# Cumulated decays of a gated delta rule: spread by four-row matmuls on four row tiles, subtracted on ScalarE, masked on GpSimd, two chunks earlier

## What is computed

```python
gcum = jnp.cumsum(gc, axis=-1)
idx = jnp.arange(c)
tril = idx[:, None] >= idx[None, :]
diff = gcum[..., :, None] - gcum[..., None, :]
decay = jnp.where(tril, jnp.exp(jnp.where(tril, diff, 0.0)), 0.0)
a_mat = jnp.where(strict, jnp.einsum("bhnid,bhnjd->bhnij", kb, kc) * decay, 0.0)
intra = jnp.einsum("bhnid,bhnjd->bhnij", qc, kc) * decay
```

## Time and profile before

| | |
|---|---|
| runs | 581.05, 581.10, 581.26 us; median 581.1 |
| profiled execution | 581.15 us, its span 579.3 us |
| TensorE busy | 568.1 us, 98% of the span |
| VectorE busy | 382.2 us, 66% |
| ScalarE busy | 299.0 us, 52% |
| GpSimd busy | 78.2 us, 13% |

### The profile page before, as it was taken

How to read it: one execution, slowest core, us unless ns; L and a number is a source line. 1 busy time by engine, 2 the same in 40 slices (tenths; PEclk the granted TensorE clock), 3 DMA queues, 4 the chain that set the end, 5 groups by cost and what they waited for, 6 DMA issues and landing times.

```text
span 579.3 us, 10011 instructions
## 1 busy us (share of the span) xinstructions
PE 568.1 (98%) x4010; PEld 504.7 (87%) x4010; DVE 382.2 (66%) x612; ACT 299.0 (52%) x470; POOL 78.2 (13%) x93
## 2 busy tenths in 40 slices
PE   9999999999999999989999999999999999999997
PEld 8999999899788999878888888898788888888886
DVE  4778898855666652977754573757766566566664
ACT  5569555515435456647464634366454544545542
POOL 4011210761600000163321000000000000000000
PEclk9999999999999999999999999999999999999999
DMA  8954477595755425433443455565466756667631
GB/s 255 256 179 142 151 189 248 98 301 175 208 148 163 137 83 192 146 107 112 152 141 116 146 176 202 162 193 168 145 188 178 216 177 187 185 180 217 167 125 72
DMA packets 101432, 98.25 MB, mean 170 GB/s; under 512 B 4819, under 2 KB 87816, under 8 KB 101387
## 3 DMA queue, kind: packets, MB, share of 16 engines
q1 hardware_dynamic: 99072, 93.69, 52.8%
q0 software_dynamic: 1808, 2.78, 2.7%
q10 hardware_dynamic: 506, 1.14, 0.6%
HBM read 96.46 MB, written 1.84 MB: 170 GB/s over the span
## 4 chain that ended last, share of the span: by engine, by line
PE 88%; DVE 6%; issue 3%; ACT 2%; POOL 1%; DVEq 0%; ACTq 0%; POOLq 0%
PE ps L1423 18%; PE ps L1425 17%; PE ps L1424 17%; PE ps L1521 13%; PE ps L1524 6%; PE ps L1601 4%; PE ps L1428 4%; PE ps L1441 2%; DVE w_lo L944 2%; PE ps L1498 2%; PE ps L1756 1%; PE ps L1730 1%; PE ps L1632 1%; ACT w_hi L623 1%; DVE cacc L1039 1%
## 5 line engine op out<-in xcount | busy, mean ns | idle before, releaser
L944 DVE TENSOR_TENSOR w_lo<-raw,w_hi 128x2048 fp32r<-128x2048 f32 x76 | 176.3, 2319 | 99.2 <-ACT w_hi L623 99.0
L623 ACT ACTIVATE w_hi<-raw 128x2048 fp32r<-128x2048 f32 x76 | 145.3, 1912 | 81.5 <-PE ps L1425 75.2
L1521 PE MATMUL ps<-h_both,w_hi 128*128 128x512 f32 x352 | 122.8, 397 | 1.0 <-DVE w_lo L944 0.6
L1423 PE MATMUL ps<-h_both,w_hi 128*128 128x256 f32 x352 | 101.7, 289 | 0.7 <-DVE h_both L970 0.3
L1424 PE MATMUL ps<-h_both,w_hi 128*128 128x256 f32 x352 | 99.5, 283 | 0.0
L1425 PE MATMUL ps<-h_both,w_lo 128*128 128x256 f32 x352 | 99.5, 283 | 0.0
L1524 PE MATMUL ps<-h_both,w_lo 128*128 128x256 f32 x352 | 91.1, 279 | 0.0
L1521 PEld LDWEIGHTS ps<-h_both,w_hi 128*128 128x128 f32 x352 | 63.9, 188 | 15.1 <-issue 3.2
L1423 PEld LDWEIGHTS ps<-h_both,w_hi 128*128 128x128 f32 x352 | 67.3, 191 | 5.0 <-issue 4.8
L1524 PEld LDWEIGHTS ps<-h_both,w_lo 128*128 128x128 f32 x352 | 66.4, 189 | 3.3
L1424 PEld LDWEIGHTS ps<-h_both,w_hi 128*128 128x128 f32 x352 | 67.4, 192 | 0.0
(11 more groups left out here) (359 smaller groups left out, 965.6 us busy)
## 6 DMA issues: line engine op xcount, KB each, us to landing
raw<-in_w_in SPq DMA_DIRECT2D x31, 1024.0 KB, 5.2
raw<-in_w_gate SPq DMA_DIRECT2D x22, 512.0 KB, 4.0
raw<-in_w_up SPq DMA_DIRECT2D x22, 512.0 KB, 5.3
raw<-in_w_down SPq DMA_DIRECT2D x11, 1024.0 KB, 4.9
raw<-in_cmp_w SPq DMA_DIRECT2D x8, 1024.0 KB, 6.3
raw<-in_w_proj_a SPq DMA_DIRECT2D x4, 1024.0 KB, 5.3
raw<-in_w_proj_b SPq DMA_DIRECT2D x4, 1024.0 KB, 5.1
raw<-in_w_out SPq DMA_DIRECT2D x4, 1024.0 KB, 5.1
```

What stands on the lines that cost most here:

```text
L623: nc.scalar.activation(w_hi[s % NSPL][:], raw[RAW_OF[n]][:], ACT.Copy).then_inc(hi_done, 1)
L944: nc.vector.tensor_tensor(w_lo[s % NSPL][:], raw[RAW_OF[n]][:], w_hi[s % NSPL][:].bitcast(f32), ALU.subtract).then_inc(lo_done, 1)
L1423: pe.matmul(bank, lhs(lh), rhs(rh), start=start, stop=False)
L1521: cross = lambda stop: pe.matmul(banks[part][:], hi[:, k, part * P:(part + 1) * P], h_both[:, :, k, :], start=(k == 0), stop=stop)
```

## The change

Five things change together.

1. **Sums as rows.** `decay_columns` gets four more matmuls, each with a group's four columns of `g` as the stationary side and `upper` as the moving one. They leave the cumulated decays of four problems as rows, at partitions 32b to 32b+3 of `ps7`. VectorE copies them into `gc_rows` with four copies, in slot 6.
2. **Spreading.** The stage `row` moves from half 1 of slot 12 to half 1 of slot 10, behind the sums of squares. Its sixteen matmuls now have four rows each: a column of `sel4` (ones and zeros) repeated 128 times, and `gc_rows`. Group b uses the rows 32b and up of the array and a bank of its own (`row_ps`, banks 2 to 5), and the groups take turns, the quarter q being the outer loop.
3. **Difference.** It moves from VectorE to ScalarE: sixteen activations, Relu with scale -1 and the column `gc` as bias. The exponential takes scale -1 in turn, and stands in slot 12 between the SiLU of chunk 10 and that of chunk 11, behind `decay_factors`.
4. **Mask.** `negmask` is gone, with its load. GpSimd multiplies `ET` with `upper`, four products, ahead of the bias rows' transfer; the scaling waits for them.
5. `stage_columns` on VectorE now follows the convolution of chunk 11.

Core of the diff:

```diff
-STAGE_AT = {("kc", 0, 1): "row", ("vc", 0, 0): "kt", ("vc", 0, 1): "vt", ...
+STAGE_AT = {("gv", 2, 1): "row", ("vc", 0, 0): "kt", ("vc", 0, 1): "vt", ...
...
-            sp.dma_start(negmask[:], c_negmask).then_inc(const_in, 16)
...
+            for b in range(NB):
+                pool.wait_ge(et_ready, b + 1)
+                nc.gpsimd.tensor_tensor(problems(ET, b), problems(ET, b), upper[:].unsqueeze(1).to_broadcast([P, 4, P]), ALU.mult).then_inc(et_masked, 1)
             pool.wait_ge(conv_done, 12)
...
             for b in range(NB):
-                pool.wait_ge(et_ready, b + 1)
+                pool.wait_ge(et_masked, b + 1)
...
+            def decays():
+                for b in range(NB):
+                    wait_use(act, "row", b)
+                    nc.scalar.activation(problems(ET, b), problems(ET, b), ACT.Exp, scale=-1.0).then_inc(et_ready, 1)
...
                     if name == "row":
-                        act.wait_ge(done, u // GRING + 1)
-                        nc.scalar.activation(problems(ET, b), problems(ET, b), ACT.Exp).then_inc(et_ready, 1)
+                        act.wait_ge(g_mm, u + 1)
+                        rows4 = row_ps[b][:].rearrange("p (q c) -> p q c", q=4)
+                        for q in range(4):
+                            ins = nc.scalar.activation(problems(ET, b)[:, q, :], rows4[:, q, :], ACT.Relu, scale=-1.0, bias=pcol("gc", b)[:, q:q + 1])
+                        ins.then_inc(done, 1)
...
-                for k in {FIRST_STAGE_SLOT: [n - 2, n - 1]}.get(n, [n - 2] if 2 <= n < FIRST_STAGE_SLOT else []):
-                    conv_step(k)
+                if 2 <= n <= FIRST_STAGE_SLOT:
+                    conv_step(n - 2)
+                if n == FIRST_STAGE_SLOT:
+                    decay_factors()
+                    decays()
+                    conv_step(n - 1)
...
             def decay_factors():
                 dve.wait_ge(pre_pe, 5)
+                for b in range(NB):
+                    nc.vector.tensor_copy(gc_rows[32 * b:32 * b + 4, :], ps[7][32 * b:32 * b + 4, 0:P]).then_inc(rows_cum, 1)
...
-                    if name == "row":
-                        for q in range(4):
-                            ins = nc.vector.scalar_tensor_tensor(problems(ET, b)[:, q, :], b4[:, q, :], pcol("gc", b)[:, q:q + 1],
-                                                                 negmask[:], ALU.subtract, ALU.add)
-                        ins.then_inc(done, 1)
-                        if b == NB - 1:
-                            stage_columns()
...
                     if (n, half) == (FIRST_STAGE_SLOT, 0):
                         conv(n - 1)
+                        stage_columns()
...
+                for b in range(NB):
+                    last = pe.matmul(ps[7][32 * b:32 * b + 4, 0:P], pcol("g", b), upper[:], start=True, stop=True)
                 last.then_inc(pre_pe, 1)
...
+            def decay_rows():
+                pe.wait_ge(rows_cum, NB)
+                pe.wait_ge(sel_done, 1)
+                for q in range(4):
+                    for b in range(NB):
+                        group = slice(32 * b, 32 * b + 4)
+                        last = pe.matmul(row_ps[b][:, q * P:(q + 1) * P], sel4[group, q:q + 1].to_broadcast([4, P]), gc_rows[group, :],
+                                         start=True, stop=True)
+                        if q == 3:
+                            last.then_inc(g_mm, 1)
...
-                    if name == "row":
-                        pe.wait_ge(pre_dve, 5)
-                        if b == 0:
-                            pe.wait_ge(rk_ready, 1)
-                        for q in range(4):
-                            last = mm(q, pcol("g", b)[:, q:q + 1].to_broadcast([P, P]), upper[:])
```

More of the change, by code:

```diff
@@ L288, in hybrid_block @@
         csum_n = at("csum_n", cursor[0] - 2 * KB, [P, 2 * SEQ])
-        ident, upper, negmask = own("ident", [P, P]), own("upper", [P, P]), own("negmask", [P, P])
+        ident, upper, gc_rows = own("ident", [P, P]), own("upper", [P, P]), own("gc_rows", [P, P])
         vcz = at("vcz", yb_at + 12 * KB, [P, 4, DH])
@@ L1574, in head_sums @@
                     if j == 2:
+                        wait_use(pe, "row", NB - 1)
                         pe.wait_ge(nq_sq, 4)
@@ L1592, in head_sums @@
                     last.then_inc(csum_tr, 1)
+            def decay_rows():
[8 more added lines that the diff above has]
+                            last.then_inc(g_mm, 1)
             def gdn(name):
+                if name == "row":
+                    decay_rows()
+                    return
                 for b in range(NB):
```

24 lines of the change are left out of this document (11 added, 13 removed).

## The result

The changed kernel takes **587.75 us** (587.67 to 588.0) against 581.1 (581.05 to 581.26): ratio 1.0112, 95% interval 1.0098 to 1.0125, slower by 6.65 us. The profiled execution has a span of 585.9 us, 6.6 more than before.

What follows compares the result with a forecast made beforehand. TensorE, busy 568.1 of 579.3 us, was taken as the bound. Added work and stalls 1 and 2, less 3.81 us, left it 1.9 us behind; masks and stall 3 made 5.7: 581.1 + 5.7 = 586.8 us, range 583.2 to 589.8.

Steps and rivals of the forecast that it cites:

- The slack of chunk 12, and the split behind sixteen activations: ScalarE before chunk 12: 4.2 us of activations make its high part 6.2 us late against a slack of 1.6.
- TensorE's own costs: TensorE: 0.35 us added in slot 6; row stage 1.2 us (ends 0.95 and 3.8) in place of 3.81.
- Stalls 1 and 2: TensorE waits 3.1 us before chunk 12 for its split, and 1.05 us before chunk 13 for VectorE.
- The masks and the port: VectorE's last convolution beside GpSimd's masks: SBUF port shared, 0.79 us lost per product, 3.2 for four.
- Stall 3: Before chunk 14: TensorE waits 1.2 us for GpSimd's `flat`, out at 117.9, so chunk 14 is 5.7 us late.
- The table loads that I cost at nothing: ScalarE: load back to SiLU, 1.28 us, and one before the compressed branch's softmax; both hidden, 1.3 us if the latter uncovered.
- Two sums of the rivals: Forecast totals for the free port, 583.8 us, and for the faster case, 1.3 us gained, 579.8 us.
- the port doesn't bind: Rival at the last convolution: VectorE and GpSimd run side by side, total 583.8 us; chance 0.15.
- The row tiles run one after another: Rival in TensorE's row stage: no overlap, everything 2.6 us later, total 589.4 us; chance 0.08.
- The clock: Rival on TensorE: clock falls behind a 3.1 us stall, losing 2.5 us, total 589.3 us; chance 0.09.
- Faster: Rival at ScalarE: four banks cleared inside chunk 12's slack, 1.3 us gained, total 579.8 us; chance 0.03.

Runs made afterwards that it cites:

- r1_split_first: Changed kernel with the sixteen activations moved on ScalarE behind chunk 12's high part and the SiLU of chunk 9: 582.46 us, ratio 1.0022.
- r4_group_order: Changed kernel with the sixteen row matmuls in group order, four on one row tile and then four on the next: 587.63 us, ratio 1.011.
- r5_keep_clock: Changed kernel with fifteen identity matmuls added in TensorE's wait before the last four transposes of the keys: 586.73 us, ratio 1.0098.
- r9_chain_first: r6 with GpSimd's clearing of DTb and scalings of kn put behind the transfers out of the diagonal blocks: 578.82 us, ratio 0.9965.
- r3_mask_as_write: Changed kernel with GpSimd's four mask products replaced by four memsets of a free tile, so another output: 585.52 us, ratio 1.0073.
- r2_no_mask: Changed kernel with GpSimd's four mask products left out, so another output: 582.97 us, ratio 1.0036.
- r8_masks_last: Changed kernel with GpSimd's order alone changed: scalings of two groups, `flat`, then masks and the other scalings: 585.53 us, ratio 1.0076.
- r11_tiles_only: Kernel before with the row tiles alone, stage still in slot 12, VectorE subtracting and adding negmask: 581.07 us, ratio 0.9999.
- r6: Changed kernel with both the split ahead of the activations (r1_split_first) and GpSimd's order of r8_masks_last: 581.33 us, ratio 1.000.
- r10: r9_chain_first with the row stage back in slot 12, ScalarE still subtracting: 582.27 us, ratio 1.0021.

## Why the prediction was right, point by point

The forecast was 586.8 us; measured 587.75, inside the range and on the side named. Of the 0.95 us between them 0.6 is chunk 14 (6.3 us late, not 5.7), and 0.24 the later first chunk of the profiled execution, which no step of mine has. Its steps:

- **The slack of chunk 12, and the split behind sixteen activations.** Right: 4.25 us of activations (4.2 said), the high part from 92.39 (92.7), chunk 12 at 96.91 (97.0). r1_split_first shows it as the main cause.
- **TensorE's own costs.** Slot 6: 0.23 us instead of 0.35 (head sums at 57.60 before, 58.07 after, less 0.24 of the later start). Row stage: chunk 11 starts 1.10 us behind its first record, 34 ns a record (1.2 and 38 said). Together they put chunk 11 1.47 us later than before, counted from the first chunk (1.55 said). The Trainium skill's two rules had given 0.95 and 3.8; r4_group_order shows that the parallel one ("TensorEngine Tiling (Array Packing)", Key Properties) holds where tiles take turns, while four matmuls in a row on one tile cost more than twice as much.
- **Stalls 1 and 2.** 2.62 and 0.83 us (3.1 and 1.05 said): both too large. Less the 0.24 of the later start, chunk 12 was ready at 96.67, not 97.0, and wanted at 94.05, not 93.9. Up to chunk 13 the kernel was 1.5 us behind, not 1.9.
- **The masks and the port.** The mechanism was right, and this is the term that was mis-sized: a GpSimd product costs VectorE 1.04 us, not 0.79. Four of the six steps took 1.48 to 1.51 us instead of 0.47, and the whole 4.1 us more, not 3.2. The 1.26 us step of the earlier trace rows was a poor measure, as GpSimd's square had begun 0.5 us before it; a step that comes up while a product starts waits for the whole of it (1.01 us). Convolution 11 took 6.55 us, not 5.6. So the last transposes were 4.8 us behind, not 4.4.
- **Stall 3.** This step failed in form. TensorE did not wait for `flat`: behind the 3.87 us wait its clock fell, the half chunk took 1.5 us longer, and it reached chunk 14 at 118.86, 0.25 after `flat` was out at 118.61. r5_keep_clock shows that without the fall the wait is there, 1.23 us, where I had said 1.2. Chunk 14 was 6.3 us late instead of 5.7. Of the 0.6, 0.5 is `flat`, out at 118.61, or 118.37 without the later start, where I had said 117.9: the longer convolution, less what stalls 1 and 2 were too large. That the clock's 1.5 us fell where I had a wait of 1.2 us, and so hardly changed the sum, is luck: my sum had no clock in it.
- **The table loads that I cost at nothing.** Right. The one before the SiLU ends at 105.10, while the convolution runs until 110; the next one stands at 203.93, and from chunk 14 to the end nothing is lost (467.0 us in both).
- **Two sums of the rivals.** They are off by 0.1 us: the free port's 1.8 and 0.8 us make 583.7, and 3.81 less 1.2, 0.35 and 1.05 is a gain of 1.2, 579.9 us. Neither changes a chance or the range.

Of the rivals, *the port doesn't bind* is out (6.55 against 2.46 us). *The row tiles run one after another* is out at 34 ns a record; whether its 589.4 us was a right price stays untested, since r4_group_order's longer stage cost nothing in an order that hands ScalarE its first bank early. *The clock* did fall, but my price of 2.5 us on top of all else was wrong: a fall took 1.5 us, and what it costs is what lies beyond the wait that comes next. *Faster*, at the point that I named, would have asked for cheaper activations; r1_split_first takes away the waits before chunks 12 and 13 by their place instead, and r9_chain_first, which builds on it, is faster.

What stays open: why the clock fell behind 2.61 us before chunk 12 in some profiled executions (r3_mask_as_write, r5_keep_clock) and not in others with the same wait (the changed kernel, r2_no_mask, r8_masks_last). And the 0.5 us of TensorE's late phase by which r11_tiles_only's profile is longer than that of before is below what these runs can tell.

## What to carry over

When work moves to an engine that is mostly idle, look at the instruction that stands behind it in that engine's queue and at its slack: sixteen cheap activations ahead of a split with 1.6 us of slack cost 5.3 us, and with the same sixteen one place further back neither chunk behind them waits. Keep GpSimd instructions that read SBUF away from VectorE's two-input steps when VectorE is late, and follow a gain to the end of the program: in r6 it was given back 40 us on by a chain of transfers that GpSimd's new order had put off by 7.6 us. A stall's price and a slower clock's are not added up but laid over each other: each counts only by what it exceeds the wait behind it. The same holds for a longer stage if the next engine can start before the stage ends.

## What the runs showed of the hardware

- Four-row matmuls with 128 columns on four row tiles, taking turns: 34 ns a record (1.10 us for 32). One tile four times running, then the next: about 86 ns (2.75 us for 32).
- A GpSimd product of 128x512 with two SBUF tiles: 1.01 us alone, 1.44 to 2.43 us beside VectorE's two-input steps, which take 1.48 to 1.51 us instead of 0.47. Both pay, in turns.
- A GpSimd instruction that only writes leaves such steps at 0.47 us, but a VectorE TENSOR_SCALAR of 48 columns with one SBUF input took 1.44 us beside it instead of 0.18.
- The granted clock went to 0.50 behind waits of 3.87 us (after and r4), 3.18 (r1), 2.81 (r8), 2.61 (r3 and r5), 2.60 (r6), 2.12 (r10) and 1.88 (r3). It stayed at 1.00 behind 2.61 or 2.62 us in the profiles of the changed kernel, r2 and r8. Where the same half chunk can be compared (after, r1, r3), a fall cost 1.5 us of TensorE's work, and the time only what the next wait didn't take.
